# Flow-matching layer on one core: new orders of the opening, the column sums and the low halves, and two substitution batches solved as one

## The chip, the cores and the metric

The kernel runs on one core of one Trainium2 chip. The metric is the device time of one execution in microseconds (us). The engines are TensorE (PE, matmuls; its weight loads are PEld), VectorE (DVE), ScalarE (ACT), GpSimd (POOL) and SyncE (SP), whose queue issues most of the DMAs.

## The reference, cut to what matters

One layer is applied to a context of 128 tokens and to 512 latent tokens, with the same weights: SwiGLU, a mixer, SwiGLU, each behind an RMS norm with scale and shift made from a conditioning vector. Half of the mixer is a gated short convolution, half a bidirectional gated delta rule with four heads. All is float32.

```python
mod = silu(c) @ w_ada + b_ada                    # 9 vectors of 1024, for c and for c_ctx
h = rmsnorm(x, norm_ffn1) * (1 + sc1) + sh1
x = x + 0.5 * gt1 * ((silu(a) * b) @ w_out)      # a, b = split(h @ w_in), 2816 each
h = rmsnorm(x, norm_mix) * (1 + sc2) + sh2
proj = h @ w_mix_in                              # conv parts, q k v, z, gates
lmat = strict_lower((k * beta) @ k.T * decay)    # per chunk, head and direction
tmat = inverse(eye + lmat)
# per chunk: v_new = u - w @ s;  o = qg @ s + qk @ v_new;  s = s * g_last + kg.T @ v_new
x = x + gt2 * (concat(y_conv, rmsnorm(o) * silu(z)) @ w_mix_out)
# then the second SwiGLU and a final rmsnorm
```

## The kernel before, in words

**Tiling.** All 640 tokens stand side by side along the free dimension, as five blocks of 128 (NC = 5); the 1024 features are eight tiles of 128 partitions (KD = 8). A product of float32 quality is made of three float32r matmuls: each operand is split in a high half (w_hi, made by ACT in split_hi, L1393) and a low half (w_lo = w_raw - w_hi, made by DVE in split_lo, L1976), and PE does hi*hi, hi*lo, lo*hi, each on 2 x 320 tokens. A *unit* is one such product for 128 output features. The raw weights of a unit (w_raw), its high and its low half have two slots each, so unit u uses slot u % 2, and a load (load_w, L485) waits for lo_ready, the count of low halves.

**The order of the work.** Each engine has its own written-out list of instructions; semaphores tie them together, and nothing reorders them. The list runs: opening, six pairs of units of the first SwiGLU, further gate blocks by a seven-product scheme (L909), the output stage, 28 units of the mixer's input, the chunk loop, the mixer's output, and the second SwiGLU.

**Opening.** first_pair (PE, L856 and L881) does units 0 and 1 together. tile(k, b, units) is feature tile k on token half b. Between the tiles stand the steps that make the modulation vectors: quarter_step (L819), half_step (L809) and ada_turn (L829). Tiles 0 to 3 of h need the gains from quarters 0 and 1, tiles 4 to 7 those from quarters 2 and 3. gained_hi (ACT, L1452) and gained_lo (DVE, L2037) make h_hi and h_lo; both stand behind both splits. normed (DVE L2086, ACT L1493) makes the normed input of the later scheme; four of its eight tiles stand in the first pair, four in the second.

**Column sums.** The other five ninths of the modulation are made on DVE and ACT: column_first (ACT, L1621) starts one of five accumulations, column_sum(n) (DVE, L2285, two instructions) adds one weight row block; load_columns (SP, L509) brings it, into two buffers, and waits until sum n - 2 is done. Sums 1 to 7 stand in the pairs of units. Sums 8 to 39 stand in swiglu_out, the output stage: its eight blocks j have three units each, and SUMS_AT gives, in order, the (block, unit) slots that hold them. PE's column_rows(c) (L837) waits for all sums of a column: it stands behind blocks 2, 4, 5 and 6.

**Substitution.** The inverse of a 128x128 chunk matrix starts from its 16x16 diagonal blocks, inverted by back substitution on DVE: sub_start masks them (L2450 to L2453), sub_rows does one row in two linked instructions (multiply L2461, reduce L2464), sub_end copies the transpose (L2469). A batch holds the blocks of two chunks: batch 0 is chunks 0 and 1, batch 1 is 2 and 3, batch 2 is 4. The blocks come by pack (SP, L610) from a scratch tensor in memory, and go back by unpack (L619); load_sel (L627) brings them as the selection of a chunk, load_lt (L636) its matrix. Batches 0 and 1 are solved within the mixer's last units. Batch 2 starts in unit 27 and ends in chunk 1 of the loop.

**Chunk loop.** For n = -1 to 4 PE mixes the levels that build the inverse of chunk n + 1 (level_x L1068, level_tr L1081, turn_r L1090) with the state products of chunk n (v_product L1177, s_product L1184, o_product, w_product L1166). DVE does update (L2491), rows_add (L2498), w_add (L2627), new_v (L2635), v_less (L2651), o_out; POOL does mask (L2861), expand (L2852) and keys (L2873) out of the selection, and at the end the low halves yc_lo (L2908). tokens(t) (PE, L1051) and tok(t) bring keys and values to token order. The iteration n = -1 is the passage from the units to the loop: it starts with unit 27 being evicted (scaled, L2045), and acc_wait(A_MO // 2, 1) on PE waits for that eviction. Behind the loop stand the sums of squares (L1210) and the first pair of units of the mixer's output (L1284).

## Time and profile before

| | us |
|---|---|
| Median of 3 runs | 1334.44 |
| The 3 runs | 1328.74, 1334.44, 1338.57 |
| The profiled execution | 1331.63 |
| Its span in the trace | 1329.7 |
| PE busy in it | 1296.4 (97%) |
| DVE, ACT, POOL busy | 927.7, 559.5, 89.6 |

Times of the trace are counted from the start of the span. Busy time of PE counts each matmul until its modelled end, so that it includes pipelining. A bracket at the end of a row of a timeline is the idle time of that engine just before the row, and what ended it.

### The profile page before, as it was taken

What the parts mean: (1) busy time and instruction counts of PE and PEld (TensorE: products, weight loads), DVE (VectorE), ACT (ScalarE), POOL (GpSimd) and SP (SyncE); (2) the same over time, 40 slices, a digit from 0 to 9 for tenths busy, and PEclk for the clock granted to TensorE, in tenths of its full rate; (3) what the DMA queues carried; (4) which work ended last, traced back from release to release, by engine and by line L of the source; (5) the groups of instructions that cost most, each with busy time, mean ns of one, the idle gap of its engine ahead of it and who ended that gap; (6) DMA issues with size and microseconds to landing.
All of it is one profiled execution on the core that took longest, in us unless ns stands there. A gap on an engine that the chain in (4) does not pass through costs nothing.

```text
span 1329.7 us, 23870 instructions
## 1 busy us (share of the span) xinstructions
PE 1296.4 (97%) x9131; PEld 1271.9 (96%) x9131; DVE 927.7 (70%) x1561; ACT 559.5 (42%) x927; POOL 89.6 (7%) x70
## 2 busy tenths in 40 slices
PE   6999999999999999999999899999999999999997
PEld 5889999999999999999999799999999999999997
DVE  5568888778888764666788879547978877862223
ACT  6414544345432235644323454336534334542223
POOL 0000000000000000001323564000000000000000
PEclk8999999999998999999999999999999999999999
DMA  9771423322467633212645352131322332222223
GB/s 371 265 270 33 116 75 95 95 64 84 153 204 206 196 83 87 79 48 61 183 135 149 109 150 84 52 108 48 96 77 82 95 89 68 75 74 74 72 74 137
DMA packets 223316, 153.45 MB, mean 115 GB/s; under 512 B 22493, under 2 KB 206086, under 8 KB 222214
## 3 DMA queue, kind: packets, MB, share of 16 engines
q1 hardware_dynamic: 221620, 151.55, 37.6%
q8 instruction: 55, 0.90, 0.3%
q10 hardware_dynamic: 1618, 0.81, 0.2%
q14 instruction: 23, 0.19, 0.0%
HBM read 140.41 MB, written 11.93 MB: 115 GB/s over the span
## 4 chain that ended last, share of the span: by engine, by line
PE 84%; DVE 9%; DMA 3%; ACT 2%; issue 1%; SPq 1%; DVEq 0%; ACTq 0%
PE ps L747 38%; PE ps L909 32%; PE ps L1298 3%; DMA cw_raw<-in_w_ada 2%; DVE cw_acc L2285 2%; PE ps L1357 1%; DVE sub_tmp L2461 1%; DVE w_lo L1976 1%; DMA ada_w<-in_w_ada 1%; PE ps L1284 1%; PE ps L1081 1%; DVE sub_x L2464 1%; PE ps L856 1%; ACT hf L1493 1%; PE ps L1068 1%
## 5 line engine op out<-in xcount | busy, mean ns | idle before, releaser
L1393 ACT ACTIVATE w_hi<-w_raw 128x1024 fp32r<-128x1024 f32 (+1 forms) x106 | 108.4, 1023 | 338.7 <-PE ps L747 282.7
L1976 DVE TENSOR_TENSOR w_lo<-w_raw,w_hi 128x1024 fp32r<-128x1024 f32 (+1 forms) x106 | 125.3, 1183 | 106.9 <-ACT w_hi L1393 103.6
L747 PE MATMUL ps<-h_hi,w_hi 128*128 128x320 f32 x736 | 173.3, 317 | 2.3 <-DVE w_lo L1976 2.3
L747 PE MATMUL ps<-h_lo,w_hi 128*128 128x320 f32 x736 | 170.1, 312 | 0.0
L747 PE MATMUL ps<-h_hi,w_lo 128*128 128x320 f32 x736 | 169.7, 312 | 0.0
L747 PE MATMUL ps<-g_hi,w_hi 128*128 128x320 f32 x660 | 152.6, 313 | 2.7 <-DVE w_lo L1976 2.7
L747 PE MATMUL ps<-g_lo,w_hi 128*128 128x320 f32 x660 | 151.4, 311 | 0.0
L747 PE MATMUL ps<-g_hi,w_lo 128*128 128x320 f32 x660 | 151.3, 311 | 0.0
L747 PEld LDWEIGHTS ps<-h_hi,w_hi 128*128 128x128 f32 x736 | 123.9, 190 | 6.6 <-issue 6.4
L909 PE MATMUL ps<-T_hi,S_hi 128*128 128x320 f32 x408 | 126.0, 309 | 0.0
L909 PE MATMUL ps<-T_hi,S_lo 128*128 128x320 f32 x408 | 126.0, 309 | 0.0
L909 PE MATMUL ps<-T_lo,S_hi 128*128 128x320 f32 x408 | 125.9, 309 | 0.0
L747 PEld LDWEIGHTS ps<-h_hi,w_lo 128*128 128x128 f32 x736 | 125.1, 190 | 0.0
L747 PEld LDWEIGHTS ps<-h_lo,w_hi 128*128 128x128 f32 x736 | 124.9, 190 | 0.0
L747 PEld LDWEIGHTS ps<-g_hi,w_hi 128*128 128x128 f32 x660 | 111.0, 189 | 4.6 <-DVE w_lo L1976 2.9
L747 PEld LDWEIGHTS ps<-g_lo,w_hi 128*128 128x128 f32 x660 | 111.4, 189 | 0.0
L747 PEld LDWEIGHTS ps<-g_hi,w_lo 128*128 128x128 f32 x660 | 111.3, 189 | 0.0
L2285 DVE SCALAR_TENSOR_TENSOR cw_acc<-cw_raw,silu_c,cw_acc 128x1024 f32<-128x1024 f32 x70 | 86.2, 1279 | 22.9 <-DMA cw_raw<-in_w_ada 20.5
L909 PE MATMUL ps<-B_hi,A_hi 128*128 128x320 f32 x264 | 81.5, 309 | 0.5 <-issue 0.5
L909 PE MATMUL ps<-B_lo,A_hi 128*128 128x320 f32 x264 | 81.4, 308 | 0.0
L909 PE MATMUL ps<-B_hi,A_lo 128*128 128x320 f32 x264 | 81.4, 308 | 0.0
L1566 ACT ACTIVATE sa<-ps 128x320 f32<-128x320 f32 x34 | 14.9, 438 | 153.5 <-PE ps L909 153.5
(369 smaller groups left out, 2745.9 us busy)
## 6 DMA issues: line engine op xcount, KB each, us to landing
w_raw<-in_w_ffn_in SPq DMA_DIRECT2D x50, 512.0 KB, 3.8
cw_raw<-in_w_ada SPq DMA_DIRECT2D x40, 512.0 KB, 4.4
w_more<-in_w_ffn_in SPq DMA_DIRECT2D x34, 512.0 KB, 4.5
ada_w<-in_w_ada SPq DMA_DIRECT2D x16, 1024.0 KB, 9.4
w_raw<-in_w_ffn_out SPq DMA_DIRECT2D x34, 448.0 KB, 3.4
w_raw<-in_w_mix_in SPq DMA_DIRECT2D x28, 512.0 KB, 3.8
w_raw<-in_w_ffn_out SPq DMA_DIRECT2D x17, 512.0 KB, 3.5
w_raw<-in_w_mix_out SPq DMA_DIRECT2D x8, 512.0 KB, 3.5
```

Source lines behind the costliest of these rows:

```text
L747: last = pe.matmul(to[a_slot][b], w, m[:, k0 + k, part[b]], start=start and k == 0 and n == 0, stop=stop and k == kt - 1 and n == 2)
L856: pe.matmul(accw[s][b], w, m[:, k, PARTW[b]], start=k == 0 and n == 0, stop=k == KD - 1 and n == 2)
L909: last = pe.matmul(to, a, m[:, k, :], start=not again and k == 0 and n == 0, stop=k == 3 and n == 2, skip_group_check=again)
L1068: last = pe.matmul(hs(ps[6] if n == 0 and m < 2 else x_bank, h), NT[(3 * n + m) % 2][:, h, :], (Tm if m else Tc0)[:, h, :], start=True, st ...
L1081: last = pe.matmul(hs(u_bank, h), Xm[:, h, :], (rc_of(n, m - 1) if m else Rc0)[:, h, :], start=True, stop=True)
L1284: last = pe.matmul(acc[s][b], w, m[:, k % 4, PART[b]], start=k == 0 and n == 0, stop=k == KD - 1 and n == 2)
L1298: last = pe.matmul(acc[s][b], w, m[:, k % 4, PART[b]], start=k == 0 and n == 0, stop=k == KD - 1 and n == 2)
L1357: last = pe.matmul(to[:, 0:t1 - t0], w, m[:, k0 + k, t0:t1], start=start and k == 0 and n == 0, stop=stop and k == k1 - k0 - 1 and n == 2)
L1393: nc.scalar.activation(w_hi[:, slot, 0:kt * P], w_raw[:, slot, 0:kt * P], ACT.Copy).then_inc(hi_ready, 1)
L1566: nc.scalar.activation(c11, X, ACT.Silu).then_inc(act_ev, 1)
L1976: nc.vector.tensor_tensor(w_lo[:, slot, 0:kt * P], w_raw[:, slot, 0:kt * P], w_hi[:, slot, 0:kt * P].bitcast(F32), ALU.subtract).then_inc( ...
L2285: nc.vector.scalar_tensor_tensor(out=to[:, i, :], in0=raw_at(n)[:, :], scalar=silu_c[:, k, i:i + 1], in1=to[:, i, :], op0=ALU.mult, op1=AL ...
```

## The change

It has seven parts. None of them changes a number that is computed.

1. *Opening, PE*: tiles 0 and 1 of unit 0 come ahead of the third quarter step, those of unit 1 behind it. The fourth quarter step stands behind tile 2, token half 1 of tiles 0 and 1 ahead of tile 4, tile 7 behind the third turn. ACT and DVE make two tiles of h behind each of the two splits, where they made four behind both.
2. *Pairs*: normed does 3 and 5 tiles, where it did 4 and 4; column sum 3 moves from the second pair to the third.
3. *Output stage*: block 2 loses a slot for a sum, block 6 gets one; in block 5 one moves from the second unit to the third.
4. *Substitution*: batches 1 and 2 are solved together, with twice the elements in each instruction. Their tiles lie in slot 0 of w_raw, so the two first loads of the mixer's output weights move into the chunk loop. Rows and ends of both batches stand ahead of chunk 0, none in the chunk loop proper. Batch 2 gets an input tile of its own, cleared by POOL, and POOL's first Rc0 waits for it. pack(1) and pack(2) stand behind the load of unit 25, unpack(1) ahead of chunk 2's selection, unpack(2) at the end of iteration 0.
5. PE's wait for the eviction of unit 27 moves from behind tokens(2) to behind tokens(4). tok(0) moves up a unit.
6. *Low halves*: that of U_MO moves from iteration 3 to iteration 4.
7. POOL's low halves yc_lo wait for the last rows_add.

```diff
 place["at"] += 2 * 4 * KF * T
+at_wraw = place["at"]
 w_raw = sb("w_raw", [P, 2, KD * P], F32)
...
-x_of = (sub["x"], sb("sub_x1", [P, BS, BS], F32, at=at_ssq + 1024), sb("sub_x2", [P, BS, BS], F32, at=at_ssq))
+xx = sb("sub_xx", [P, 2, BS, BS], F32, at=at_ssq)
+neg2, tmp2 = (sb(n, [P, 2, BS, BS], F32, at=at_wraw + 2048 * i) for i, n in enumerate(("sub_n2", "sub_tmp2")))
+u_of = (sub["u"], sub["u"], sb("sub_u2", [P, BS, BS], F32, at=at_g + 36 * B + 8192))
+x_of = (sub["x"], xx[:, 0, :, :], xx[:, 1, :, :])
+xt_of = (sub["xt"], sub["xt"], sub["u"])
...
 summed = lambda n: (cp_rdy, 2 * (n // KD) + 2) if n % KD == 0 else (ac_rdy, 14 * (n // KD) + 2 * (n % KD))
-SUMS_AT = tuple((j, b) for j in range(1, 7) for b, m in enumerate((1, 2, 2 if j < 5 else 1)) for _ in range(m))
+SUMS_AT = tuple((j, b) for j in range(1, 7) for b, m in enumerate((1, 1 if j in (2, 5) else 2, 2)) for _ in range(m))
 slot_of = {n: SUMS_AT[7 * (n // KD - 1) + max(n % KD - 1, 0) - (1 if n % KD == 0 and n > KD else 0)]
...
     m, size = 16 * chunks_of(b), P * HEADS * BS * chunks_of(b)
-    src = x_of[b] if (part == 0) == (d == 1) else sub["xt"]
+    src = x_of[b] if (part == 0) == (d == 1) else xt_of[b]
     if part < 2:
...
-        if b > 0:
-            sp.wait_ge(u_read, b)
+        if b == 1:
+            sp.wait_ge(u_read, 1)
         sp.wait_ge(st_lt, 16 * (3, NC, NC)[b])
...
                 p0 = 64 * d + m * odd
-                sp.dma_start(sub["u"][p0:p0 + m, :, :], view(d_lt[b, odd * (BS * P + BS):], [
+                sp.dma_start(u_of[b][p0:p0 + m, :, :], view(d_lt[b, odd * (BS * P + BS):], [
                     [2 * (BS * P + BS), m], [P, BS], [1, BS]])).then_inc(pk_in, 16)
...
             pack(0)
-        if g == 9:
+        if n == 25:
             pack(1)
+            pack(2)
         if n == 27:
...
             load_sel(0)
-            pack(2)
         if n == 18:
...
     w_mo_v = w_mo[0].rearrange("(k p) f -> p k f", p=P)
-    for j in range(2):
-        load_w(U_MO + j, j % 2, w_mo_v[:, :, P * j:P * j + P], KD)
-
     load_sel(1)
-    unpack(1)
     sp.wait_ge(mm_done, U_MO)
...
     for n in range(NC - 1):
-        if n == 2:
-            unpack(2)
+        if n == 0:
+            unpack(1)
+            for j in range(2):
+                load_w(U_MO + j, j % 2, w_mo_v[:, :, P * j:P * j + P], KD)
         if n + 2 < NC:
...
         load_o(n + 1, 1)
+        if n == 0:
+            unpack(2)
     for j in range(2, KD):
...
     spread(0)
-    quarter_step(2, 0)
...
-        for b in range(2):
-            pe.wait_ge(lo_ready, b + 1)
-        between = {0: lambda: quarter_step(3, 1), 1: lambda: ada_turn(1, 1), 5: lambda: half_step(4, 0),
-                   6: lambda: half_step(5, 1), 7: lambda: half_step(6, 2)}
-        for k in range(KD):
+        def first(k, units=(0, 1)):
             pe.wait_ge(h_rdy, k + 1)
-            tile(k, 0)
-            if k in between:
-                between[k]()
+            tile(k, 0, units)
+
+        pe.wait_ge(lo_ready, 1)
+        first(0, (0,))
+        first(1, (0,))
+        quarter_step(2, 0)
+        pe.wait_ge(lo_ready, 2)
+        first(0, (1,))
+        first(1, (1,))
+        first(2)
+        quarter_step(3, 1)
+        first(3)
+        ada_turn(1, 1)
         tile(0, 1)
+        tile(1, 1)
+        first(4)
+        half_step(4, 0)
+        first(5)
+        half_step(5, 1)
+        first(6, (0,))
+        half_step(6, 2)
         half_step(7, 3)
-        tile(1, 1)
+        first(6, (1,))
         ada_turn(2, 2)
+        first(7)
         pe.wait_ge(gain_rdy, 3)
...
             tokens(2)
-            acc_wait(A_MO // 2, 1)
         elif more:
...
                 tokens(4)
+                acc_wait(A_MO // 2, 1)
             level_x(nx, 2)
...
         split_hi(u, u, KD, 0, first=True)
-    for k in range(4):
-        gained_hi(0, k)
+        for k in range(2 * u, 2 * u + 2):
+            gained_hi(0, k)
     ada_out(1, P)
...
-    swiglu_in(0, U_F1I, A_F1I, SA0[0], early=lambda: [normed(0, k) for k in range(4)])
-    swiglu_in(1, U_F1I, A_F1I, SA0[0], lambda: column_first(0), early=lambda: [normed(0, k) for k in range(4, KD)])
+    swiglu_in(0, U_F1I, A_F1I, SA0[0], early=lambda: [normed(0, k) for k in range(3)])
+    swiglu_in(1, U_F1I, A_F1I, SA0[0], lambda: column_first(0), early=lambda: [normed(0, k) for k in range(3, KD)])
     swiglu_in(2, U_F1I, A_F1I, SA0[0])
...
         split_lo(u, u, KD)
-    for k in range(4):
-        gained_lo(0, k)
+        for k in range(2 * u, 2 * u + 2):
+            gained_lo(0, k)
     first_gains(1)
...
-    swiglu_in(0, column_tools, early=lambda: [normed(0, k) for k in range(4)])
-    swiglu_in(1, lambda: (column_sum(2), column_sum(3)), mid=lambda: column_sum(1),
-              early=lambda: [normed(0, k) for k in range(4, KD)])
-    swiglu_in(2, lambda: column_sum(5), mid=lambda: column_sum(4))
+    swiglu_in(0, column_tools, early=lambda: [normed(0, k) for k in range(3)])
+    swiglu_in(1, lambda: column_sum(2), mid=lambda: column_sum(1),
+              early=lambda: [normed(0, k) for k in range(3, KD)])
+    swiglu_in(2, lambda: (column_sum(4), column_sum(5)), mid=lambda: column_sum(3))
     swiglu_in(3, lambda: column_sum(7), mid=lambda: (ada_cols(3, 16, 4), column_sum(6)))
...
+    def both_start():
+
+        dve.wait_ge(pk_in, 64 * 3)
+        dve.wait_ge(lo_ready, U_MI + 27)
+        mask, half = sub["mask"], P // 2
+        for i in range(2):
+            u = u_of[i + 1]
+            nc.vector.tensor_tensor(neg2[0:half, i, :, :], u[0:half, :, :], mask[0:half, :, :], ALU.mult)
+            last = nc.vector.tensor_tensor(neg2[half:P, i, :, :], u[half:P, :, :].rearrange("p a b -> p b a"),
+                                           mask[half:P, :, :], ALU.mult)
+        last.then_inc(u_read, 1)
+        nc.vector.tensor_scalar(xx[:, 0, :, :], mask[:, :, :], 0.0, None, ALU.max)
+        link(nc.vector.tensor_scalar(xx[:, 1, :, :], mask[:, :, :], 0.0, None, ALU.max))
+
+    def both_rows(j1, j0):
+
+        for j in range(j1, j0 - 1, -1):
+            w = BS - 1 - j
+            link(nc.vector.tensor_tensor(
+                tmp2[:, :, 0:w, 0:w], neg2[:, :, j:j + 1, j + 1:BS].to_broadcast([P, 2, w, w]),
+                xx[:, :, j + 1:BS, j + 1:BS].rearrange("p b k i -> p b i k"), ALU.mult))
+            link(nc.vector.tensor_reduce(xx[:, :, j, j + 1:BS], tmp2[:, :, 0:w, 0:w], mybir.AxisListType.X, ALU.add))
+
     def sub_end(b=0):
-        if b > 0:
-            dve.wait_ge(st_sel, b * SEL_ST)
-        nc.vector.tensor_copy(sub["xt"][:, :, :], x_of[b][:, :, :].rearrange("p a b -> p b a")
+        if b == 1:
+            dve.wait_ge(st_sel, SEL_ST)
+        nc.vector.tensor_copy(xt_of[b][:, :, :], x_of[b][:, :, :].rearrange("p a b -> p b a")
                               ).then_inc(solved, 1)
...
                                         ).then_inc(qn_rdy, 1)
-        if n == 26:
-            tok(0)
         if n == 27:
...
             tok(1)
-            sub_rows(1, 0, 1)
-            sub_end(1)
+            both_rows(2, 2)
             rows_add(0)
-            sub_start(2)
-            sub_rows(BS - 2, 11, 2)
         dve.wait_ge(mm_done, U_MI + n + 1)
...
         if n == 24:
-            sub_start(1)
-            sub_rows(BS - 2, 9, 1)
+            both_start()
+            both_rows(BS - 2, 9)
         if n == 25:
-            sub_rows(8, 4, 1)
+            tok(0)
+            both_rows(8, 5)
         if n == 26:
-            sub_rows(3, 2, 1)
-        if n == 27:
-            sub_rows(10, 8, 2)
+            both_rows(4, 3)
...
             o_add(1)
+            split_lo(U_MO, 0, KD)
             split_lo(U_MO + 1, 1, KD)
...
                 tok(2)
-                sub_rows(7, 7, 2)
             update(nx, 1)
-            if n == 3:
-                split_lo(U_MO, 0, KD)
             if n < 0:
                 tok(3)
-                sub_rows(6, 6, 2)
+                both_rows(1, 1)
             else:
...
                     v_less(nx, d)
-                if n < 2:
-                    sub_rows((4, 1)[n], (3, 1)[n], 2)
         if n > 0 and not o_first(n, 0):
...
                 tok(4)
+                both_rows(0, 0)
             w_add(nx)
             if n < 0:
-                sub_rows(5, 5, 2)
+                sub_end(1)
+                sub_end(2)
             if n == 3:
...
             o_out(n, 1)
-        if n == 0:
-            sub_rows(2, 2, 2)
-        if n == 1:
-            sub_rows(0, 0, 2)
-            sub_end(2)
-
...
     for g in range(2, GROUPS_DN):
+        if g == GROUPS_DN - 1:
+            nc.gpsimd.memset(u_of[2][:, :, :], 0.0)
         decayed_qk(*divmod(g, 2))
...
             pool.wait_ge(tr_mm, 3 * n - 2)
+        if n == 0:
+            pool.wait_ge(u_read, 2)
         expand(Rc0, n, 1).then_inc(lev_rdy, 1)
...
         pool.wait_ge(kg_rdy[d], NC - 1)
+    pool.wait_ge(e_rdy, 2 * NC)
     for k in range(4):
```

## Rows read from the trace of the kernel before

**Rows 1.** The page, parts 1 and 2; clock in tenths over 40 slices.

```profile
PE 1296.4 (97%) x9131; PEld 1271.9 (96%) x9131; DVE 927.7 (70%) x1561; ACT 559.5 (42%) x927; POOL 89.6 (7%) x70
PEclk8999999999998999999999999999999999999999
```

**Rows 2.** PE's waits, one row: us in total, times, longest.

```profile
PE ps L747 <- DVE w_lo L1976: 5.0, 4, 2.7
```

**Rows 3.** Timeline of the opening (start, length), then windows (clock behind POOL).

```profile
18.79 2.36 DVE L1976 TENSOR_TENSOR w_lo<-w_raw,w_hi 128x1024 fp32r<-128x1024 f32 x2
19.61 3.71 ACT L1452 ACTIVATE h_hi<-x,gain 128x128 fp32r<-128x128 f32 x8
21.90 1.93 PE L819 MATMUL ps<-ada_w,ccol 128*32 128x128 f32 x32 [3.23 <-DMA ada_w<-in_w_ada]
30.59 0.41 PE L856 MATMUL ps<-h_hi,w_hi 128*128 128x320 f32 x1 [1.00 <-DVE h_lo L2037]
49.65 0.53 PE L747 MATMUL ps<-h_hi,w_hi 128*128 128x320 f32 x2 [0.70 <-DVE w_lo L1976]
...
21.70:25.10 3.40, 3.20 (x37) 2.72 (x38) 3.14 (x7) 1.62 (x4) 0.00 (x0) 0.53 1.04 420
```

**Rows 4.** Timeline, third pair of units: DVE's column sum, and PE.

```profile
72.56 2.48 DVE L2285 SCALAR_TENSOR_TENSOR cw_acc<-cw_raw,silu_c,cw_acc 128x1024 f32<-128x1024 f32 x2 [5.01 <-DMA cw_raw<-in_w_ada]
78.30 0.54 PE L747 MATMUL ps<-h_hi,w_hi 128*128 128x320 f32 x2 [0.96 <-DVE w_lo L1976]
```

**Rows 5.** Timeline of the output stage, DVE and PE, then windows.

```profile
413.65 2.48 DVE L2285 SCALAR_TENSOR_TENSOR cw_acc<-cw_raw,silu_c,cw_acc 128x1024 f32<-128x1024 f32 x2 [3.54 <-DMA cw_raw<-in_w_ada]
418.48 0.90 PE L747 MATMUL ps<-g_hi,w_hi 128*128 128x320 f32 x2 [2.66 <-DVE w_lo L1976]
471.35 2.47 DVE L2285 SCALAR_TENSOR_TENSOR cw_acc<-cw_raw,silu_c,cw_acc 128x1024 f32<-128x1024 f32 x2
475.22 1.13 DVE L2302 SCALAR_TENSOR_TENSOR x<-ps,gate,x 128x128 f32<-128x128 f32 x3 [1.39 <-PE ps L747]
...
417.90:424.70 6.80, 6.22 (x23) 6.22 (x24) 6.77 (x12) 0.94 (x2) 0.00 (x0) 0.50 0.70 217
```

**Rows 6.** DVE's groups by form, 590 to 830 us: busy us, mean ns.

```profile
L2461 DVE TENSOR_TENSOR sub_tmp<-sub_n,sub_x 128x121 f32<-128x121 f32 x3 | 3.1, 1036 | 0.1
L2461 DVE TENSOR_TENSOR sub_tmp<-sub_n,sub_x 128x225 f32<-128x225 f32 x3 | 1.9, 620 | 0.1
L2461 DVE TENSOR_TENSOR sub_tmp<-sub_n,sub_x 128x4 f32<-128x4 f32 x3 | 0.5, 166 | 0.1
L2464 DVE TENSOR_REDUCE sub_x<-sub_tmp 128x15 f32<-128x225 f32 x3 | 1.2, 387 | 0.1
```

**Rows 7.** Timeline of the substitution, 700 to 751 us: SP, PE, DVE.

```profile
702.37 6.76 SPq L485 DMA_DIRECT2D w_raw<-in_w_mix_in  x3
708.88 0.53 PE L747 MATMUL ps<-h_hi,w_hi 128*128 128x320 f32 x2 [0.66 <-DVE w_lo L1976]
739.06 0.89 DVE L2045 TENSOR_TENSOR pn<-ps,rinv 128x320 f32<-128x320 f32 x2
748.08 1.40 DVE L2627 TENSOR_TENSOR W<-R,ps 64x512 f32<-64x512 f32 x2 [2.11 <-PE ps L1081]
740.01 1.16 PE L1081 MATMUL ps<-Rc,Xm 128*128 128x128 f32 x8 [3.05 <-DVE pn L2045]
```

**Rows 8.** Second chunk, POOL and PE; landing of selections at 723 us.

```profile
761.95 2.36 POOL L2873 TENSOR_TENSOR kg<-ktok,s_kgs 128x512 f32<-128x512 f32 x2
767.29 1.06 PE L1184 MATMUL ps<-VN,kg 128*128 128x128 f32 x8
DMA to landing us min/median/max: 3.9/4.4/4.8
```

**Rows 9.** Timeline of the loop's end: DVE's low half, PE's sums.

```profile
816.08 1.21 DVE L1976 TENSOR_TENSOR w_lo<-w_raw,w_hi 128x1024 fp32r<-128x1024 f32 x1
817.93 1.84 PE L1210 MATMUL ps<-ones,osq 128*128 128x1 f32 x16
```

## The prediction

> **What bounds the kernel now.** I read the page first: TensorE (PE) is busy for 97% of the span, and its clock is granted in full in nearly every slice [rows 1]. The reader is to see that no other engine can be the bound over the whole kernel: what an edit of order can win is the 33 us in which PE is idle, plus the stretches at half clock. So I read next who PE waits for, and then the timeline around each wait. In the waits one group stands out, PE waiting for VectorE's (DVE's) low half of the weights [rows 2]. In the timeline its four places are 49.65, 78.30, 418.48 and 708.88 us [rows 3, 4, 5, 7]. The other waits that the change touches are for the third modulation quarter at 21.90 and for h_lo at 30.59 [rows 3], and for an eviction at 740.01, 3.05 us [rows 7]. The rest of PE's idle time (the start of the program, its last output) is not touched. In all sums below a us of PE is a us of the kernel, a us of DVE only where PE waits for it.
>
> The profiled execution took 1331.63 us for a span of 1329.7. The sum is made against it. It lies 2.8 us under the median of the three runs, 1334.44, and I carry the sum over to the median as a ratio.
>
> **1. The opening.** PE idles 3.23 us up to 21.90, and ScalarE makes h_hi only behind both splits, DVE h_lo behind both low halves [rows 3]. The two low halves take 2.36 us together, so w_lo of unit 0 stands at 18.79 + 1.18 = 19.97. ScalarE's tiles take 3.71 / 4 = 0.93 us each, and with one split (about 1 us) ahead of them instead of two they begin near 18.7. The first h_lo then stands at about 20.9 and the second at 21.9. What moves into PE's wait is one tile of one unit, three matmuls, and three more delay the third quarter by about 0.85 us. The stretch from 21.70 to 25.10 runs at 0.53 of the clock [rows 3], and I leave that stretch where it is, so three matmuls fewer in it are worth 0.8 us. The wait of 1.00 us at 30.59 stays: the fourth quarter, and with it the gains of tiles 4 to 7, come some 1.1 us later, and tiles (0,1) and (1,1), now ahead of tile 4, only fill that. Tile 7 behind the second turn covers the 0.9 us in which PE waited for DVE's shift columns, and half steps 6 and 7 are next to each other, which saves some 0.3 us of switching. Together 2.0. The wait of 0.70 at 49.65 [rows 3] is for a split that ScalarE makes behind four normed tiles; with three ahead (1.1 us each, estimated from the pace of the h tiles, which are slightly shorter) it goes: 0.7. Late next is the load of the last half step; it is issued when quarter 4 is done, about 1 us later than now, and is wanted 1 us earlier. Sum -2.7. Bounds: -0.7 if the last load is late, -4.4 if the half-clock stretch (3.4 us, costing 1.7) doesn't come.
>
> **2. The pairs of units.** At 78.30 PE waits 0.96 us because column sum 3 waits 5.01 us for its transfer in front of the split of unit 5 [rows 4]. That sum moves one unit on, behind the split. Sums 4 and 5 are then both in the second half of the third pair, where PE has a whole unit and an adaLN step (some 9 us) before it needs the next split; two sums are 5 us. Sum -1.0, bounds 0 and -1.0.
>
> **3. Sums in the output stage.** DVE's sum at 413.65 waited 3.54 us for its transfer, the split behind it came late, PE waited 2.66, and the 6.80 us behind ran at a clock of 0.50: another 3.4 us [rows 5]. With one sum fewer in column block 2 each later sum stands a slot further back than the transfer it needs: following the sums one by one (2.48 us each, a transfer issued when the sum two before it is done, about 4.4 us to land) I get the split some 3 us before PE wants it. -6.1. The sum taken away there comes back in block 6, last slot, and PE's column_rows behind block 6 waits for the last sum of all. Now that sum ends with 1.39 us to spare [rows 5]. One sum more is 2.48, so PE waits 1.1, and 0.4 more because sum 38's transfer, issued when sum 36 is done, may not have landed. +1.5, bounds 0 and +4.9 (with a half-clock stretch of 3.4 behind this wait as well). Sum -4.6.
>
> **4. Substitution.** A row of a batch is a multiply and a reduce. Between 4 and 225 elements the multiply goes from 166 to 620 ns and the reduce ends at 387 [rows 6], so about 0.16 + 2.0 ns an element and 0.15 + 1.05 ns. Over 15 rows (1240 elements) that is 4.9 + 3.6 + 1 of gaps = 9.5 us a batch. The pair does 2480 elements in the same 30 instructions: 7.4 + 4.9 + 1 = 13.2, against 19. That is some 6 us less of DVE, but none of it sits now behind the first update of the chunk loop, so DVE has about as much to do before the loop as it had. Bounds of the pair: 13 us, and 19 if nothing is shared.
> What PE gains is order. (a) The weights of unit 25 no longer wait in SP's queue behind the packing of batch 1 (702.37, three loads): the 0.66 at 708.88 goes [rows 7]. (b) tok(0) comes one unit earlier: 0.45. (c) The eviction of unit 27 (739.06) stood behind the start and four rows of batch 2, and PE waited for it 3.05 us ahead of level_tr, though it needs the bank only at level_x(0, 2) [rows 7]. With the wait moved there and the rows gone, the last unit ends near 734.0, and level_tr(0, 1) follows near 736 instead of 740.01. (d) Four waits of 0.2 to 0.8 us behind it lose 0.9 together. So W of chunk 0, at 748.08 now [rows 7], would be ready 5.1 us earlier. Against that, rows 1 and 0 of the pair stand just ahead of it on DVE, while GpSimd (POOL) is at work: +1.0. -4.1, bounds -5.1 and -1.
> The multiplies of 121 elements took 1036 ns on the mean, longer than those of 225 elements with 620 [rows 6]; in the timeline the long ones lie beside a POOL instruction, and reduces are not stretched. The Trainium skill (SBUF — State Buffer, Who interferes with whom) states it as an exclusive lock that a DVE instruction with two SBUF inputs and a POOL instruction take in turns. By that rule a batch that has fewer but longer multiplies pays the lock fewer times, and the trace agrees so far; the +1.0 is from the row's 1036 against the 410 that the line through the other sizes gives, one and a half such waits.
> (e) In the chunk loop SP now does unpack(1), eight stores, and two loads of 512 KB ahead of the selection for chunk 2. A selection behind such loads took 3.9 to 4.8 us to land [rows 8]. I get it landing near 756, and POOL's chain behind it 5.1 us later against PE than now. Now POOL's first key product is ready at 763.1 and PE takes it at 767.29 [rows 8]: 4.2 us of slack. PE waits 0.9 to 1.1. unpack(2) does the same to chunk 3, where the slack is about 5, and there it hides. +1.1, bounds 0 and +5. (f) The low half of U_MO now stands at the loop's end, 1.21 us, ahead of the sum that PE's second sum of squares (the second eight of 817.93) waits for [rows 9]: +1.0. POOL's low halves behind e_rdy no longer stretch rows_add, where PE waited 0.3: -0.3. Nobody waits for them before 819. Costed at nothing: POOL's clearing of batch 2's input, in one of its idle stretches of 8 us between the products of the units; POOL's wait for u_read ahead of Rc0 (DVE reads the inputs near 714, Rc0 is due behind 722); and the two packings, 4 us of SP's queue ahead of the load of unit 26, which lands near 708.5 where its split is due at 711. If that last cover were gone, PE would wait for the split of unit 26 from 715.4 on. Sum of part 4: -4.1 + 1.1 + 0.7 = -2.3, bounds -5 and +4.
>
> **The sum**: -2.7 - 1.0 - 4.6 - 2.3 = -10.6 us, 1321.0 for the profiled execution; times 1334.44 / 1331.63 it is 1323.8. The forecast's own range is 1319 to 1328.
>
> **The rivals.**
> A. More is won: the half-clock stretch of the opening is not there (-1.7), PE waits neither for the last column sum (-1.5) nor in chunk 1 (-1.1). For it: 3.23 us of idle PE ahead of that stretch become 2.3. Against: nothing in the order forbids those waits. -14.9: 1319.5.
> B. DVE gives it back: the pair costs 19 us instead of 13, which puts W of chunk 0 some 3 us later, and the new wait behind block 6 brings a half-clock stretch, 3.4. For it: the wait of 2.66 had one behind it [rows 5]. Against: the wait of 3.05 at 740 had none. -4.2: 1330.2.
> C. The wait in the output stage only moves: the sums are bound by transfers of 4 us with two buffers, and with the order changed another split is late by as much, again with half clock. For it: 3.54 us of DVE's idle time are for a transfer [rows 5]. Against: 28 sums of 2.48 are 69 us in six blocks of 19.4. -10.6 + 6.1 = -4.5: 1329.9.
> D. Slower: the selections of chunks 2 and 3 come so late that POOL's chain sets the chunk loop's pace. From a landing at 755 on each us is one of PE's. If the stores and weight loads ahead keep each selection back 6 us more than I reckon, that is 6 + 6 us, -10.6 + 12 = +1.4: 1335.8. For it: SP works its queue in order, and load_lt and load_o stand behind the same wait. Against: the stores are small, and one selection behind such loads landed in 4.8 [rows 8].
>
> **How the numbers follow.** Forecast 0.50, A 0.20, B 0.13, C 0.11, D 0.06. The likeliest is 1323.8. The range takes in A and B and leaves out D and A's lower end: 1316 to 1332. About 1% is what a measurement of this kernel tells from no change, that is, below 1321.1 or above 1347.8. A lies wholly below, and about a quarter of the forecast's own range: 0.20 + 0.13 = 0.33. Above lies only the far end of D: 0.02. The rest, 0.65, is within 1%.
>
> **What would show it.** In the changed profile: PE's first h matmul near 21.0, the first wide unit near 47 and no wait at the split of unit 5; no wait in front of block 4 and a full clock there; a wait of 1 to 2 us before column_rows behind block 6; no eviction wait at the first level_tr; pair multiplies of 225 x 2 elements of about 1.08 us; POOL idle before chunk 2's selection and a PE wait of about 1 us at its key product. Wrong would be: a wait of over 3 us in the output stage (C), a pair of over 18 us (B), or PE idle for more than 4 us between the first v_product and the last (D).

## The result, and the profile after

The changed kernel takes 1325.95 us, median of 8 runs (1325.1 to 1327.75), the kernel before 1331.65 in the same comparison (8 runs, 1328.74 to 1338.57). The ratio is 0.9944, with an interval of [0.9923, 0.9966]: faster by half a per cent, and within the 1% that I had called no change. The quotient of the two medians is 0.9957, 5.7 us. The forecast was 1323.8. The profiled execution took 1326.6 us for a span of 1324.8, against 1331.63 for 1329.7 before: 5.0 us less, where the sum had said 10.6.

The page says how little of this a share of busy time can show:

```profile
span 1324.8 us, 23839 instructions
PE 1296.3 (98%) x9131; PEld 1272.2 (96%) x9131; DVE 924.0 (70%) x1531; ACT 560.5 (42%) x927; POOL 88.8 (7%) x71
...
PEclk8999999999999999999999998999999999999999
```

PE's busy time is the same as in [rows 1]; of the clock's row, the 8 in the thirteenth slice is a 9 again, and a new 8 stands in the 25th. The reading has to go by waits and by clock, place by place. PE executes the same 9131 matmuls in both kernels, from 41 us on in the same order, so I set the start of the same matmul in one trace against the other. How much earlier the changed kernel is:

| at (us, before) | earlier by | what changed since the line above |
|---|---|---|
| 49.65, first wide unit | 2.05 | the opening |
| 78.30, split of unit 5 | 3.09 | the pairs, 1.04 |
| 424.75, behind the split of block 4 | 8.3 | wait of 2.66 now 0.19, half-clock stretch gone |
| 475.33, column rows | 7.4 | a new wait of 0.87 |
| 580, in the units of the mixer's input | 8.9 | a half-clock stretch of 3.4 us at 574.9 is not there, 1.5 |
| 708.88, split of unit 26 | 9.7 | the wait of 0.66 gone |
| 749.02, W of chunk 0 | 12.15 | the eviction wait of 3.05 gone, 1.54 new |
| 767.29, key product of chunk 1 | 9.7 | POOL late |
| 810, in the last chunk | 10.7 | waits of 0.10 and 0.31 gone, and smaller gains |
| 818.74, inside the second sum of squares | 9.7 | 0.81 new |
| 826, and from there to the end | 4.9 | a new half-clock stretch of 10.2 us |

The timeline of PE after, at the places that answer to [rows 3], [rows 4] and [rows 5] (start, length, instruction, idle before it and for whom):

```profile
21.09 0.39 PE L860 MATMUL ps<-h_hi,w_hi 128*128 128x320 f32 x1 [2.42 <-DVE h_lo L2055]
22.88 1.94 PE L824 MATMUL ps<-ada_w,ccol 128*32 128x128 f32 x32
47.60 0.53 PE L752 MATMUL ps<-h_hi,w_hi 128*128 128x320 f32 x2
75.22 0.58 PE L752 MATMUL ps<-h_hi,w_hi 128*128 128x320 f32 x2
412.96 0.56 PE L752 MATMUL ps<-g_hi,w_hi 128*128 128x320 f32 x2 [0.19 <-DVE w_lo L1994]
467.96 1.07 PE L842 MATMUL ps<-cw_acc,pick 128*32 128x256 f32 x16 [0.87 <-DVE cw_acc L2303]
```

The stretch that went at 574.9, in the kernel before (windows as in [rows 3]):

```profile
574.90:578.30 3.40, 3.40 (x15) 3.40 (x14) 2.97 (x12) 1.80 (x2) 0.00 (x0) 0.50 0.54 153
```

The third quarter (22.88) no longer has a wait in front of it; the wide unit and the split of unit 5 stand without one, block 4 with 0.19 instead of 2.66. In the substitution, against [rows 7] and [rows 8]:

```profile
724.09 0.63 PE L1108 MATMUL ps<-ident,Re 128*128 128x128 f32 x4 [1.54 <-DVE Re L2532]
728.14 1.02 PE L1099 MATMUL ps<-Rc,Xm 128*128 128x128 f32 x7
736.87 1.35 PE L1195 MATMUL ps<-vtok,W 128*128 128x128 f32 x10 [0.57 <-DVE W L2662]
752.84 1.16 PE L1086 MATMUL ps<-Tc,NTa 128*128 128x128 f32 x8 [1.51 <-POOL NTa L2890]
757.61 1.13 PE L1202 MATMUL ps<-VN,kg 128*128 128x128 f32 x8 [0.94 <-POOL kg L2902]
```

The wait of 3.05 ahead of level_tr is gone (728.14 has none), and there are two for POOL. SP and POOL in the same stretch:

```profile
741.74 1.04 SPq L490 DMA_DIRECT2D w_raw<-in_w_mix_out  x2
746.00 1.30 SPq L632 DMA_DIRECT2D sel<-d_sel  x2
...
749.93 1.26 POOL L2881 TENSOR_TENSOR Tc<-sel,blk 128x512 f32<-128x512 f32 x1 [7.57 <-DMA sel<-d_sel]
```

And the end of the chunk loop, first PE's timeline, then windows (length, busy time of PE, PE's weight loads, DVE, ACT and POOL, granted clock, DMA share, GB/s):

```profile
807.24 0.95 PE L1228 MATMUL ps<-ones,osq 128*128 128x1 f32 x8
809.00 1.05 PE L1228 MATMUL ps<-ones,osq 128*128 128x1 f32 x8 [0.81 <-DVE osq L2652]
811.11 1.70 PE L1228 MATMUL ps<-ones,osq 128*128 128x1 f32 x8
...
808.00:810.00 2.00, 1.19 (x11) 1.10 (x10) 2.00 (x4) 1.05 (x2) 0.00 (x0) 1.00 1.00 285
812.00:814.00 2.00, 2.00 (x9) 2.00 (x10) 1.36 (x2) 0.69 (x1) 0.00 (x0) 0.50 0.01 2
818.00:820.00 2.00, 2.00 (x11) 2.00 (x10) 0.95 (x2) 0.34 (x1) 0.00 (x0) 0.50 0.00 0
```

The wait of 0.81 was forecast. What stands behind it was not: the granted clock falls from 1.00 to 0.50, the lower of its two levels, from 810.6 to 820.8, and eight one-column matmuls take 1.70 us instead of 0.95. That one stretch costs 4.8 of the 9.7 us that the kernel had won until then (the expectations below have it 0.3 us early, and at 4.7). One small wait of the kernel before has gone on the way there; its row:

```profile
806.35 0.66 PE L1090 MATMUL ps<-ident,Re 128*128 128x128 f32 x4 [0.31 <-DVE Re L2491]
```

Last the pair of batches on DVE, by form and by line, against [rows 6]:

```profile
L2502 DVE TENSOR_TENSOR sub_tmp<-sub_n,sub_xx 128x450 f32<-128x450 f32 x1 | 1.9, 1926 | 0.0
L2502 DVE TENSOR_TENSOR sub_tmp<-sub_n,sub_xx 128x392 f32<-128x392 f32 x1 | 0.8, 837 | 0.0
L2502 DVE TENSOR_TENSOR sub_tmp<-sub_n,sub_xx 128x242 f32<-128x242 f32 x1 | 1.6, 1615 | 0.0
...
L2502 DVE TENSOR_TENSOR sub_tmp<-sub_n,sub_xx 128x2 f32<-128x2 f32 (+14 forms) x15 | 12.6, 842 | 0.3
L2479 DVE TENSOR_TENSOR sub_tmp<-sub_n,sub_x 128x1 f32<-128x1 f32 (+14 forms) x15 | 5.6, 370 | 0.5
L2505 DVE TENSOR_REDUCE sub_xx<-sub_tmp 128x2 f32<-128x2 f32 (+14 forms) x15 | 4.9, 326 | 0.5
L2482 DVE TENSOR_REDUCE sub_x<-sub_tmp 128x1 f32<-128x1 f32 (+14 forms) x15 | 3.6, 239 | 0.5
```

### The profile page after: what moved, and what is told of

Its sections match the earlier page's. It is cut to its first block, busy times and chain, and to the rows that moved or that the text cites. A ratio compares the mean times of both kernels' runs of the same rounds, so it can differ in the third digit from the quotient of the medians.

```text
span 1324.8 us, 23839 instructions
## 1 busy us (share of the span) xinstructions
PE 1296.3 (98%) x9131; PEld 1272.2 (96%) x9131; DVE 924.0 (70%) x1531; ACT 560.5 (42%) x927; POOL 88.8 (7%) x71
## 4 chain that ended last, share of the span: by engine, by line
PE 88%; DVE 6%; issue 2%; ACT 2%; POOL 1%; DMA 1%; ACTq 0%; SPq 0%; DVEq 0%; POOLq 0%
PE ps L752 41%; PE ps L927 32%; PE ps L1316 3%; PE ps L1375 1%; PE ps L1302 1%; PE ps L860 1%; DVE sub_tmp L2502 1%; DVE w_lo L1994 1%; PE ps L1086 1%; PE ps L1099 1%; PE ps L804 1%; DVE cw_acc L2303 0%; ACT w_hi L1411 0%; PE ps L1202 0%; DVE sub_tmp L2479 0%
```

## The experiments

Twelve kernels, each timed in up to 12 runs beside the kernel before on the same chip. That kernel's own median went from 1331.1 to 1335.2 from one comparison to the next, so medians are set against each other only within a comparison, and ratios beyond it. "Late half" is whether the low half of U_MO stands at the loop's end, as in the change; the last column is the half-clock stretch behind the second sum of squares in the profiled execution.

| kernel | median | ratio to before | late half | stretch, us |
|---|---|---|---|---|
| the change | 1325.95 | 0.9944 [0.9923, 0.9966] | yes | 10.2 |
| 1 low half back | 1322.82 | 0.994 [0.9922, 0.9957] | no | 6.8 |
| 2 weights later | 1324.89 | 0.9945 [0.9923, 0.9968] | yes | 10.2 |
| 3 parts 1 to 3 on before | 1324.38 | 0.9943 [0.9918, 0.9968] | no | none |
| 4 sums alone on before | 1331.05 | 1.0 [0.9975, 1.0025] | no | 6.8 |
| 5 without POOL's wait | 1325.86 | 0.9952 [0.9937, 0.9968] | yes | 6.8 |
| 6 other slots | 1326.33 | 0.9952 [0.9934, 0.9969] | yes | 10.2 |
| 7 rows behind the update | 1326.27 | 0.9953 [0.9935, 0.9971] | yes | 10.2 |
| 8 opening and pairs on before | 1327.65 | 0.9971 [0.9953, 0.9989] | no | none |
| 9 edits 1 and 2 | 1320.79 | 0.9911 [0.9876, 0.9945] | no | none |
| 10 wide sums | 1326.24 | 0.9937 [0.9908, 0.9966] | yes | 10.2 |
| 11 edits 1, 2 and 10 | 1318.89 | 0.9895 [0.9857, 0.9934] | no | none |
| 12 late half on kernel 3 | 1329.79 | 0.9964 [0.9939, 0.9989] | yes | 6.8 |

Kernels 1 to 4, 5 to 8 and 9 to 11 shared a comparison each, kernel 12 had its own; they ran on three chips in all.

**Kernels 1 and 12: the low half of U_MO.**

```diff
-                    split_lo(U_MO, 0, KD)
                     split_lo(U_MO + 1, 1, KD)
...
                     update(nx, 1)
+                    if n == 3:
+                        split_lo(U_MO, 0, KD)
```

> The changed kernel with one part undone: the low half of U_MO is again formed in iteration 3, behind update(nx, 1), and no longer ahead of the second sum of squares. What it is for: in the changed kernel a matmul of the second sum of squares waits 0.81 us for DVE at 809.00, and right behind it the granted clock is 0.50 of full speed from 810.3 to 820.5 (10.2 us), which costs about 4.7 us; before had neither. Theory 1 (the wait beside the thin matmuls is what lets the clock fall): both go, and the time is 0.8 + 4.7 = 5.5 us under the changed kernel's 1326, about 1320.5. Theory 2 (the clock would fall there anyway, from the one-column matmuls): only the 0.8 us go, and the half-clock stretch stands between 809 and 821; time about 1325. Theory 3 (the low half is then late for the first matmuls of the output projection): a new wait for DVE of about 1 us near 818 to 822, time 1321 to 1326.

The wait of 0.81 went, and none of 0.3 us or more came in its place. Smaller ones did: 0.7 us is lost between the last chunk's start and the second sum, 0.27 of it in a wait for VN, behind the low half's new place, where the changed kernel loses 1.0 with its 0.81. So as waits the two places differ by 0.3 us. The stretch did not go in the profiled execution; it was 6.8 us instead of 10.2. PE's timeline (the sums now sixteen without a gap) and the window behind:

```profile
806.84 1.84 PE L1228 MATMUL ps<-ones,osq 128*128 128x1 f32 x16
809.51 1.18 PE L1228 MATMUL ps<-ones,osq 128*128 128x1 f32 x8
...
812.00:814.00 2.00, 2.00 (x11) 2.00 (x10) 0.00 (x0) 0.00 (x0) 0.00 (x0) 0.50 0.36 107
```

So the wait isn't needed for the clock to fall. Over all 12 runs, though, 6 had a mean clock of 0.995 or more, against 1 of 8 of the changed kernel. The median is 3.1 us lower than the changed kernel's, but in another comparison, and the two ratios (0.994, 0.9944) don't part them. Of the 3.0 us by which the profiled execution is ahead, 1.1 was won in chunk 1, where PE waited 0.33 for NTa instead of 1.51; the edit reaches nothing there. So neither theory holds as I wrote it. To see whether the late half alone brings the stretch, I moved it the other way on kernel 3, which had none there:

> The first test's edit the other way round, on a kernel that had no half-clock stretch there: the new opening, the pairs and the sums' slots on the kernel before (1324.4, no half-clock stretch behind 740), and the low half of U_MO formed ahead of the second sum of squares instead of in iteration 3; nothing else of the substitution's part. So far the profiled runs with a wait of 0.8 us ahead of the second sum of squares had the stretch 6 times out of 6 (6.8 to 10.2 us), those without it 2 times out of 7 (6.8 us). Theory 1 (the wait draws the clock down): PE waits 0.8 us for osq near 811, the granted clock is 0.50 for 6.8 to 10.2 us behind it, and the median is 3 to 5.5 us above 1324.4, at 1327.4 to 1330. Theory 2 (the late half costs only its wait, and the stretch belongs to something else in the substitution's part): 0.8 us more, 1325.2, with no stretch.

```profile
809.80 2.05 PE L1223 MATMUL ps<-ones,osq 128*128 128x1 f32 x16
...
814.00:820.00 6.00, 6.00 (x27) 5.96 (x27) 2.00 (x3) 0.73 (x2) 0.00 (x0) 0.50 0.30 90
```

Sixteen sums take 2.05 us instead of 1.84, so of the wait only 0.2 is left (PE was held up 0.5 ahead of it by something else), and still the clock is 0.50 for 6.8 us. The median of 1329.79 lies in theory 1's range, but the kernel before had its highest median, 1335.15, in this comparison. By the ratios kernel 12 is 2.1 thousandths, 2.8 us, slower than kernel 3, though the intervals overlap. That is just under theory 1's 3 us, by the clock it named but without its wait. Kernels 2 and 9 differ in the same edit alone: 0.9945 and 0.9911, 4.5 us; the change and kernel 1, by 0.5 us. In none of the three pairs do the ratios' intervals part. The clock tells more. With the late half the stretch was there in 7 profiled executions of 7, without it in 2 of 7 (kernels 1 and 4; the kernel before is the seventh). And over all runs of the three pairs:

| pair | mean clock, late half | mean clock, without | runs at 0.995 or more |
|---|---|---|---|
| change, 1 | 0.9924 | 0.9946 | 1 of 8, 6 of 12 |
| 12, 3 | 0.9912 | 0.9947 | 1 of 12, 5 of 9 |
| 2, 9 | 0.9915 | 0.9949 | 1 of 11, 5 of 7 |

A clock lower by 0.0022 to 0.0035 over a span of 1325 us is 2.9 to 4.6 us, by my estimate. That the late half makes half clock more frequent is shown; how it does, beyond its wait, is not.

**Kernel 10: are the one-column matmuls to blame?**

```diff
-ps[7][:, HEADS * i + h:HEADS * i + h + 1], osq[i % 3][:, h, :], ones[:, :],
+ps[7][:, c0:c0 + 24], osq[i % 3][:, h, :], ones[:, 0:1].to_broadcast([P, 24]),
```

> The changed kernel with the output stage's sums of squares multiplied into 24 equal columns instead of one (the first of each 24 is read). The same 40 matmuls, the same wait of 0.81 us ahead of the second sum, more columns in each. What it is for: every half-clock stretch behind 808 in the runs so far (10.2, 10.2, 6.8, 10.2 us) lies where 24 of these one-column matmuls alternate with the projection's, and it was there once without a wait. Theory 1 (the thin matmuls themselves are what lets the clock fall): the half-clock stretch goes or shrinks to 3.4 us, the sums cost at most 0.05 us more per matmul (2 us in all by the row of a 128x128 matmul at 0.22 against 0.117 as the upper bound), and the kernel is 2 to 4.7 us faster than the changed one: 1321.5 to 1324. Theory 2 (the wait and the place decide): the stretch of 10.2 us stays, and the time is 1326 to 1327.

```profile
809.76 1.07 PE L1229 MATMUL ps<-ones,osq 128*128 128x24 f32 x8 [0.78 <-DVE osq L2653]
...
812.00:820.00 8.00, 8.00 (x36) 7.96 (x37) 2.96 (x5) 1.80 (x3) 0.00 (x0) 0.50 0.28 83
```

Theory 1 falls: with 24 columns the matmuls cost the same (eight take 0.97 us at full clock against 0.95), and the stretch of 10.2 us stays.

**Kernel 2: SP's order.** The two loads of U_MO's weights move from `n == 0`, ahead of `load_sel(2)`, to the end of iteration `n == 1`.

> The changed kernel with the two loads of the output projection's first weights issued by SP at the end of iteration 1, behind the selection and the matrix of chunk 2, instead of ahead of them. What it is for: the changed kernel's POOL stands idle for 7.57 us until 749.93, when the selection of chunk 2 lands (issued at 746.00, the two weight loads ahead of it at 741.74), and PE then waits 1.51 us for NTa and 0.94 us for kg. Theory 1 (SP's queue is what makes the selection late): it is issued some 3 to 4 us earlier, POOL's idle stretch shrinks to about 4, both PE waits shrink or go, and the end of the substitution comes 1.4 to 2.5 us earlier: about 1324. Theory 2 (the selection waits for its buffer or for the unpacked pattern, not for the loads ahead of it): it is issued at about 745 as now, and nothing changes within 0.3 us. Theory 3 (the weights then come late for their split): a new wait of DVE for the load near 800 and of PE behind it, time 1327 or more.

```profile
745.37 1.01 SPq L632 DMA_DIRECT2D sel<-d_sel  x2
...
748.34 1.29 POOL L2882 TENSOR_TENSOR Tc<-sel,blk 128x512 f32<-128x512 f32 x1 [4.90 <-DMA sel<-d_sel]
```

Theory 1, at half its size: it had 3 to 4 us. This execution lost 1.0 us in its opening, so 745.37 corresponds to 744.3 in the changed kernel: issued 1.7 us earlier, landed 2.7 earlier, POOL idle for 4.90 instead of 7.57, and both of PE's waits, for NTa and kg, gone from the list of those over 0.3 us. Against the changed kernel the offset goes from -1.1 to +1.8 us across chunk 1. The selection is still not issued at once: SP waits 2.5 us for the stores of unpack(1) to land, where it waited 3.2, so theory 2 has a share. The medians (another comparison) show 1.1 of it, the ratios nothing: of what the profile shows, the measurement of the whole can't tell so little.

**Kernels 9 and 11: the edits together.**

> The changed kernel with both earlier edits: the low half of U_MO back in iteration 3, and the output projection's first weights loaded at the end of iteration 1. Against the changed kernel's profiled run the first was 3.1 us by the medians and the second took PE's waits for NTa (1.51) and kg (0.94) away. Theory 1 (they add): 1325.95 - 3.1 - 2.0 = about 1320.8, and no wait of PE of 0.3 us or more between 740 and 822. Theory 2 (the second only moves the first wait, because DVE's own chain becomes the bound): 1322.5, as the low half alone. The half-clock stretch behind the second sum of squares is open: it was there (6.8 us) without any wait in front of it in the run of the low half alone, and absent in the parts 1 to 3.

> The low half of U_MO back in iteration 3, the weights behind the selection of chunk 2, and the sums of squares over 24 columns, all on the changed kernel. Theory 1 (thin matmuls let the clock fall, and the three add): no half-clock stretch between 740 and 1310 in the profiled run, clock 0.995 or more, 1319 to 1320.5 with a scatter under 3 us. Theory 2 (they do not): like the two edits without the wide sums, 1320.5 to 1323, with a half-clock stretch of 3 to 10 us behind 806.

Kernel 9 came to 1320.79, just what theory 1 said, and kernel 11 to 1318.89. Whether the edits add isn't shown by that: singly neither moved the ratio, together they move it by 3.3 thousandths. Both are below the kernel before and below kernel 10 in the same comparison; the change itself wasn't in it, and kernel 9's interval overlaps the change's by 0.0022. Kernel 11's scatter was 5 us, where under 3 was expected. Theory 1 of kernel 9 had no wait over 0.3 us; PE still waited 0.67 for kg, and 0.58 at 819.96, as it does in the kernel before. In kernel 9's profiled execution the sums of squares stand without a wait, and the clock is full:

```profile
806.44 1.84 PE L1229 MATMUL ps<-ones,osq 128*128 128x1 f32 x16
...
808.00:814.00 6.00, 6.00 (x50) 5.99 (x50) 4.26 (x8) 2.78 (x4) 0.00 (x0) 1.00 0.37 110
```

In the same comparison kernel 9 is 5.45 us under kernel 10, which has the change's order. What the wide sums add to kernel 11, 1.9 us in the medians of 6 and 7 runs, I don't claim: alone they gave nothing.

**Kernels 3, 4 and 8: the parts on the kernel before.** Kernel 4 changes SUMS_AT alone, kernel 8 the opening and the pairs, kernel 3 all three.

> The kernel before with the new opening, the pairs of the first two units and the new slots of the output stage's sums, and none of the substitution's part: no joint solution of batches 2 and 3, low half where it was. From the changed kernel's trace these three parts are worth 7.4 to 7.7 us by column_rows(4) and block 7. Theory 1 (the parts add): the offset against before at the first matmul of the substitution is that of the changed kernel (about -8.7 with before's half-clock stretch at 574.9 gone, -7.6 with it there), and stays there to the end since nothing behind is changed: 1323 to 1324.5, some 2 us FASTER than the whole change, because the whole change gives 4.7 back in its half-clock stretch behind the second sum of squares. Theory 2 (the clock falls somewhere in the later stages here too, since it comes of the earlier start and not of the low half): a half-clock stretch of 3 to 10 us behind 800, time 1326 to 1329.

> The kernel before with the new slots of the output stage's sums alone. Theory 1: the wait of 2.66 us ahead of block 4 and the half-clock stretch of 6.8 us behind it (3.4 us lost) go together, and about 0.9 to 1.5 us come back as a new wait ahead of the rows of block 4: -4.6 us by block 7, time about 1327. Theory 2 (the half-clock stretch was not due to the wait, and went in the changed kernel because of its earlier start): the wait goes, the half-clock stretch stays, -1.2 us, time about 1330.5. The stretch of before at 574.9 (3.4 us long, 1.1 lost) is in question too: if it goes here, it hangs on the timing and not on the opening.

> The kernel before with the new opening and the pairs of the first units alone. What it is for: the four kernels with the new opening scatter by 3 to 7 us from run to run, the kernel before by 17 us over 31 runs and the sums alone by 13 us over 12. Theory 1 (the new opening takes the scatter away, since the quarter step no longer stands in PE's queue waiting for its weights, 3.23 us at 21.90 in before): this one scatters by 5 us or less, and its median lies 3.1 us (2.05 at the first wide unit and 1.0 behind unit 5) and half the scatter under the kernel before: about 1327. Theory 2 (the scatter comes from the substitution, where POOL's pieces of yc_lo hold up DVE): it stays, 10 us or more, with a median 3 us under before: about 1329.

("Batches 2 and 3" in the first of these are batches 1 and 2.) Kernel 3 came out at the upper end of its theory 1, 1324.38: no stretch behind 800, one of 3.4 us at 732, and 8.1 us earlier than before at 806 and 6.9 at the end, behind a gap of 0.98 us in PE's own queue, for which the profile shows no cause. The 2 us by which it was to beat the whole change are not there by the ratios; the three parts give as much as the whole. Its interval, like the whole's, is 0.2% wide to each side, 3 us.

Kernel 4 did in place what was expected: by block 4 it is 5.2 us earlier against before, the wait down to 0.20 and the half clock gone, 4.3 at the rows, then 3.9. Its time was not: 1331.05 and a ratio of 1.0, where theory 1 had 1327. The profiled execution ended 3.5 us later than before, and 4 above the kernel's own median, so its loss doesn't explain the median. It lost that in the last chunk, in one DVE instruction, with POOL's timeline beside it:

```profile
797.39 6.07 POOL L2908 TENSOR_TENSOR yc_lo<-yc,yc_hi 128x640 fp32r<-128x640 f32 x4
...
798.42 5.59 DVE L2498 SCALAR_TENSOR_TENSOR Re<-Rc,rows,Re 128x512 f32<-128x512 f32 x1
...
805.39 1.11 PE L1090 MATMUL ps<-ident,Re 128*128 128x128 f32 x4 [3.44 <-DVE Re L2491]
```

The addition to Re takes 0.74 us when alone. Here it ends 0.55 us after POOL's four instructions. Behind it come half-clock stretches of 3.4 us at 804.8 and 6.8 at 821.9. The Trainium skill (SBUF — State Buffer, Who interferes with whom) has an exclusive lock between a DVE instruction with two inputs in SBUF and a GpSimd one that reads SBUF. The trace agrees: 5.59 us instead of 0.74 beside POOL's four, and DVE did not get in between two of them either. Where the sums' 4.3 us went in the other runs stays open; on the new opening the same edit is worth 2.8 thousandths (kernels 3 and 8).

Kernel 8 was 0.93 us earlier than before at the first wide unit (1.1 less than the changed kernel; its half-clock stretch lay 1.3 us later in the opening) and 1.96 behind unit 5, and PE waited 2.93 us ahead of block 4. Its runs still scatter by 10.2 us, from 1325.7 to 1335.9: the opening does not take the scatter away, and theory 1 falls in that. The median is 3.4 us under before in the same comparison, against the 3.1 expected.

**Kernel 5: POOL's wait.** The line `pool.wait_ge(e_rdy, 2 * NC)` is left out of the changed kernel.

> The changed kernel without POOL's new wait for e_rdy ahead of the four pieces of yc_lo. What it is for: in the run of the sums alone (which has no such wait) POOL's four pieces ran back to back from 797.39 to 803.46, and one addition of DVE to Re that began at 798.42 took 5.59 us instead of 0.74; PE's turn_r then waited 3.44 us. Theory 1 (POOL and DVE exclude each other, and who is first is chance): here too a piece of DVE's row additions is stretched, by 1 to 5 us, PE waits 0.3 to 3.4 us for Re near 796, and the runs scatter upward: median 1326.5 to 1329, highest over 1330 (the changed kernel's eight runs lie within 1325.1 to 1327.75). Theory 2 (the wait guards nothing, because POOL's pieces now start later or earlier than the additions): the same time as the changed kernel within 0.5 us, and as narrow.

Nearer to theory 2: 1325.86, and PE never waits for Re near 796. POOL's four pieces ran 6 us earlier, and only the last of them touched an addition to Re:

```profile
788.22 6.07 POOL L2939 TENSOR_TENSOR yc_lo<-yc,yc_hi 128x640 fp32r<-128x640 f32 x4
...
793.06 1.79 DVE L2539 SCALAR_TENSOR_TENSOR Re<-Rc,rows,Re 128x512 f32<-128x512 f32 x1
```

The stall of kernel 4 was seen once, in an order without the change's part 4; where the scatter of the kernel before comes from (17 us over 31 runs) stays open.

**Kernel 6: other slots.**

```diff
-enumerate((1, 1 if j in (2, 5) else 2, 2))
+enumerate((1, 1 if j == 2 else 2, 2 if j < 6 else 1))
```

> The changed kernel with other slots for the output stage's sums: block 2 has one fewer in the middle as in the change, and the one that is still to be saved is taken from the last slot of block 6 and not from the middle of block 5. What it is for: the changed kernel's last slot of block 6 has two sums, and PE waits 0.87 us at 467.96 for the second before the column rows. Theory 1: that wait goes, the wait of 0.3 or less at 413 stays as small, no new one comes in block 5, and everything behind is 0.9 us earlier: about 1325. Theory 2 (block 5 with five sums is like block 2 before): a new wait of 1 to 2.7 us for w_lo between 440 and 470, with or without a half-clock stretch: 1326 to 1330.

Neither: PE waits 0.94 for the last sum, as before the edit. DVE's timeline, from block 6:

```profile
460.94 2.48 DVE L2303 SCALAR_TENSOR_TENSOR cw_acc<-cw_raw,silu_c,cw_acc 128x1024 f32<-128x1024 f32 x2 [0.18 <-DMA cw_raw<-in_w_ada]
463.34 1.22 DVE L1994 TENSOR_TENSOR w_lo<-w_raw,w_hi 128x1024 fp32r<-128x1024 f32 x1
465.09 2.48 DVE L2303 SCALAR_TENSOR_TENSOR cw_acc<-cw_raw,silu_c,cw_acc 128x1024 f32<-128x1024 f32 x2 [0.53 <-DMA cw_raw<-in_w_ada]
```

DVE has one sum fewer in the last slot but reaches it later, and transfers hold it up: these two, and one of 4.50 us ahead of a sum of block 5, at 442.92. Moving one sum between blocks 5 and 6 does not remove the wait.

**Kernel 7: rows 4 and 3 of the pair behind update(0, 0) and tok(1).**

> The changed kernel with the pairs of rows 4 and 3 solved behind update(0, 0) and tok(1), and no longer at the end of iteration 26. What it is for: PE's turn_r waits 1.54 us at 724.09 for Re, whose update stands in DVE's queue behind seven pairs that POOL's lock stretched (multiplies of 1.09 to 1.61 us). Theory 1: the two pairs of 3.8 us leave the queue ahead of the update; the wait goes; turn_r starts 1.5 us earlier; of that 0.5 to 1.5 us reach v_product, since the rows now stand ahead of rows_add(0) and of tok(2). Time 1324.5 to 1325.5. Theory 2 (the delay moves to rows_add(0)): PE waits as much or more for Xm or W near 734 to 737 (now 1.14 and 0.57), and the selections of chunk 1 land later: time 1326 to 1328.

Theory 2, though the wait that grew is for VN and not for Xm or W. turn_r has no wait and is 1.9 us earlier than in the changed kernel, and 16 us later that has become 0.2:

```profile
735.63 2.02 PE L1195 MATMUL ps<-vtok,W 128*128 128x128 f32 x16 [0.47 <-DVE W L2660]
739.53 1.16 PE L1202 MATMUL ps<-VN,kg 128*128 128x128 f32 x8 [0.98 <-DVE VN L2668]
```

DVE's work ahead of the loop bounds here; moved, it is late at the next readers, vtok (0.39) and VN (0.98).

## Why the prediction was right, and where it was not

The time was right, 1325.95 against 1323.8 and within the forecast's own range. The gain was not, and the time has some luck in it. The forecast was 10.6 us under a median of 1334.44; in the comparison the kernel before had 1331.65, so that only 5.7 us were gained, or 7.5 by the ratio of 0.9944, where the forecast's ratio was 0.992. In the profiled executions it was 10.6 against 5.0. The terms of the sum gave 3.1 us less than forecast (parts 1, 3 and 4), a gain of 1.5 and small ones of 0.7 came that it did not have, and one cost of 4.8 it lacked: 10.6 - 3.1 + 1.5 + 0.7 - 4.8 = 4.9.

- **Part 1, -2.7 forecast, -2.05 measured.** First h matmul at 21.09 (I had 20.9), wide unit at 47.60 without a wait. The half-clock stretch came (22.1 to 25.5), as supposed. Tile 7 took away a wait of 0.88, the neighbouring half steps gave 0.3, and the wide unit 0.6: these are nearly as I had them. What is missing is in front: the fourth quarter started 1.5 us later than before (27.05 against 25.54) where I had 1.1, and of the 0.8 for the half-clock stretch 0.3 was left.
- **Part 2, -1.0 and -1.04.** Right, with its reason.
- **Part 3, -4.6 and -4.3.** The wait of 2.66 left 0.19, the half clock left with it, 5.2 in all where I had 6.1, and the wait that comes back is 0.87 where I had 1.5. Kernel 4 shows the same 4.3 alone, in its trace. My reason for the 1.5, one sum more in the last slot, is wrong in its place: kernel 6 took that sum away and the wait stayed.
- **Not forecast: 1.5 us at 574.9.** The half-clock stretch there went in the changed kernel's profile, and so it did in kernels 1, 2, 3, 5, 6, 7, 9, 10 and 12; kernels 4, 8 and 11 have it. Nothing in the diff touches that place.
- **Part 4, (a) to (d): -4.1 and -3.3.** The waits of 0.66 and of 3.05 went as said. But update(0, 0) stood behind the six rows 8 to 3 of the pair, stretched by POOL (their multiplies took 6.9 us where my line gives 3.2), and came 1.54 late. The term that was mis-sized is the pair: I had 7.4 us for its multiplies by the line through the undisturbed sizes, and they took 12.6; the reduces took 4.9, as worked out. With 17.5 us and 0.8 of gaps the pair takes 18.3, where I had 13.2: over the 18 that I had named as the sign of rival B. The three batches of before took 19.8 + 10.8, one batch alone takes 5.6 + 3.6, which leaves 21.4 for the other two, 23.1 with their gaps: the pair saves 4.8, not 6. Its 450-element multiply took 1.93 us, where I had said 1.08, while the 338-element one, with POOL idle, took 0.76 and the 392-element one, which POOL overlapped only at its end, 0.84. The line was right for undisturbed multiplies, and charged none of the disturbed ones but the last two, with 1.0.
- **(e): +1.1 and +2.5.** The place and the cause were right; kernel 2, with SP's two weight loads moved away, has neither wait. I had taken only the key product as the first to suffer; NTa comes before it.
- **(f): +1.0 and +1.0 as a wait**, but the step left out what the clock does. I had charged half clock behind other waits (rival B, the bound of part 3) and did not ask the question here, at the one place where the wait lies among short matmuls. This is the step that failed: +4.8 in the profiled execution. Over all runs the edit cost 2.8 us by the ratios of kernels 3 and 12, 4.5 by 2 and 9 and 0.5 by 1 and the change, its wait included, each with intervals that overlap; by the mean clock it cost some 3 to 4.6. The -0.3 came: the wait of 0.31 for Re at 806.35 is gone. It didn't need POOL's new wait, for it is gone in kernel 5 too.
- **The rivals.** A did not come: each of its three costs was there. B's first half came as a price (18.3), but W was only 0.8 us later than the sum had it, not 3; its second (half clock behind block 6) did not come. C did not. D's mechanism was there at a fifth of its price.

Parts 4 to 7 as a whole give nothing that these measurements can tell: kernel 3 without them is at 0.9943, the change at 0.9944. The gain of 3.3 us before the loop is real, and is spent in the loop on POOL's late selection and on the late low half. With both undone (kernel 9) the kernel comes to 0.9911.
